# A decoder step on one core: column strips for the modulation projection, and gated-recurrence scores in two 64-token blocks

## The reference

```python
mod = jnp.einsum('bd,de->be', jax.nn.silu(c), w_ada[l]) + b_ada[l]     # 9 conditions, 1024 -> 6144
h = x * (1.0 + sc1) + sh1
...
scores = jnp.einsum('bhik,bhjk,bhijk->bhij', qi, ki, decay)            # decay = exp(b_i - b_j), j <= i
o = jnp.einsum('bhij,bhjv->bhiv', scores, vi) + jnp.einsum('bhik,bhkv->bhiv', qi * jnp.exp(b), s)
```

## Time and profile before

| | us |
|---|---|
| median of 3 runs | 2076.36 (2075.5 to 2076.95) |
| the profiled execution's own time | 2077.7 |
| its span, first to last instruction | 2075.9 |
| PE busy | 1972.5 (95%) |
| DVE busy | 696.5 (34%) |
| ACT busy | 445.5 (21%) |
| POOL busy | 420.5 (20%) |

### The profile page before, as it was taken

One profiled execution on the slowest core, in us unless ns is written; L12 is line 12 of the kernel. 1 busy time (PEld: TensorE's weight loads), 2 busy tenths in 40 slices (PEclk: granted clock), 3 DMA queues, 4 the chain that ended last, 5 costly groups with the idle time before them and its releaser, 6 DMA issues.

```text
span 2075.9 us, 24423 instructions
## 1 busy us (share of the span) xinstructions
PE 1972.5 (95%) x7628; PEld 1224.6 (59%) x7628; DVE 696.5 (34%) x1473; ACT 445.5 (21%) x946; POOL 420.5 (20%) x661
## 2 busy tenths in 40 slices
PE   6999999999999999999969999999999999999994
PEld 1754548587858757888857444444444444444443
DVE  1113980499049943000147411111111111111114
ACT  1203431344134443000021111111111111111111
POOL 0001430144014300000000612222222222222220
PEclk9899999999999989999978899999999999999997
DMA  9112432200220083311021599999999999999962
GB/s 387 41 41 85 161 127 84 81 27 19 83 81 2 4 325 123 145 59 41 9 80 62 203 388 372 362 374 364 375 362 372 358 373 368 364 372 360 377 178 93
DMA packets 56941, 419.50 MB, mean 202 GB/s; under 512 B 6289, under 2 KB 10001, under 8 KB 31145
## 3 DMA queue, kind: packets, MB, share of 16 engines
q1 hardware_dynamic: 33689, 339.44, 40.8%
q0 software_dynamic: 21456, 78.10, 14.5%
q10 hardware_dynamic: 1728, 1.05, 0.2%
HBM read 362.96 MB, written 55.61 MB: 202 GB/s over the span
## 4 chain that ended last, share of the span: by engine, by line
PE 83%; DVE 9%; ACT 3%; issue 2%; POOL 1%; DMA 1%; SPq 0%; POOLq 0%; DVEq 0%; ACTq 0%
PE ps L1023 24%; PE ps L1045 12%; PE ps L885 11%; PE ps L846 8%; PE ps L831 7%; PE ps L1014 3%; PE ps L917 3%; PE ps L776 2%; DVE work L1419 2%; PE ps L466 2%; DVE Xb L1426 1%; PE ps L802 1%; PE ps L984 1%; ACT work L572 1%; ACT work L570 1%
## 5 line engine op out<-in xcount | busy, mean ns | idle before, releaser
L1023 PE MATMUL ps<-W,work 128*128 128x512 f32 x1168 | 515.8, 595 | 1.5 <-ACT work L1206 1.2
L1023 PEld LDWEIGHTS ps<-W,work 128*128 128x128 f32 x1168 | 217.1, 191 | 247.9 <-issue 247.9
L1045 PE MATMUL ps<-work 128*128 128x512 f32 x576 | 259.1, 592 | 0.0
L1725 DVE SCALAR_TENSOR_TENSOR work<-ps,work 128x256 f32<-128x256 f32 x73 | 35.3, 484 | 514.5 <-ACT work L1212 514.5
L846 PE MATMUL ps<-Hb,W 128*128 128x260 f32 x768 | 173.4, 389 | 0.0
L1045 PEld LDWEIGHTS ps<-work 128*128 128x128 f32 x576 | 103.8, 190 | 103.3 <-issue 103.3
L846 PEld LDWEIGHTS ps<-Hb,W 128*128 128x128 f32 x768 | 148.7, 194 | 24.3 <-ACT work L1106 0.7
L1241 POOL TENSOR_TENSOR work<-work 128x128 f32<-128x128 f32 x168 | 83.0, 527 | 388.1 <-ACT work L572 388.1
L1735 DVE COPY work<-ps 128x512 f32<-128x512 f32 x144 | 99.6, 692 | 179.3 <-DMA ffrows<-work 92.5
L1311 POOL DMA_INDIRECT ffrows<-work x72 | 115.7, 1607 | 192.2 <-DVE work L1735 121.6
L831 PE MATMUL ps<-W,Hb 128*128 128x512 f32 (+1 forms) x320 | 138.4, 592 | 0.0
(11 more groups left out here) (250 smaller groups left out, 2177.0 us busy)
## 6 DMA issues: line engine op xcount, KB each, us to landing
W<-wexp SPq DMA_DIRECT2D x74, 2048.0 KB, 8.8
work<-wexp SPq DMA_DIRECT2D x73, 1024.0 KB, 8.0
W<-wq SPq DMA_DIRECT2D x36, 2048.0 KB, 8.2
work<-st_in SPq DMA_DIRECT2D x8, 1024.0 KB, 8.1
st_out<-work SPq DMA_DIRECT2D x8, 1024.0 KB, 7.3
Xb<-xT SPq DMA_DIRECT2D x2, 2080.0 KB, 17.3
h2rows<-work SPq DMA_DIRECT2D x5, 512.0 KB, 2.6
yT<-Xb SPq DMA_DIRECT2D x2, 1040.0 KB, 5.3
```

The lines of the kernel that those rows point to most:

```text
L1023: mm = pe.matmul(ps[:, k % 2, :], xe[:, k % 2, c, :], GU[:, k % 4, c, :], start=(c == 0), stop=(c == KC - 1))
L1045: mm = pe.matmul(ps[:, 4 + hf, :], aT[:, k % 2, f, :], WD[:, k, f, hf * 512:(hf + 1) * 512], start=(f == 0), stop=(f == 1))
```

## The change

- **Strips.** The 9 silu'd conditions are written into a zeroed table of 32 columns per chunk (`cond32`, in `OB`). `mod_proj` writes chunk c to partitions 32*(c%4) and up; two chunks accumulate in each of the four strips. ACT copies all 128 partitions, and `mod_turn` becomes a matmul with a 0/1 table `fold` (128x9) that adds the four strips while it turns.
- **Blocks.** The 128 tokens of a chunk are taken as two blocks of 64. Level 0 has only the corner (keys of the first block, queries of the second): one 64x64 product, which needs no mask and is copied by DVE to its place. Levels 1 to 6 and the diagonal are made for each block apart, 14 products of 64x64, each to the 64 partitions of its block. The other corner of the sum is zeroed once.
- **Layout.** The level is the innermost index of the results (in a bank: 64 tokens by 8 levels), so that a result of PE is written with a stride of 8 words, and the sum over the levels reads neighbours. A step uses bank 0 or 1 in turn, and `scores_of(n)` waits for `mask(n-2)`, no longer for `mask(n-1)`.
- The mask table shrinks from 1024 to 512 columns, the table of constants from 1930 to 1427.

```diff
 def mod_proj(n, chunks):
 ...
                 for c in chunks:
-                    mm = pe.matmul(ps[0:NCOND, mod_bank(n), :], conds[:, c, :], ring[:, q % 4, :, c, :],
-                                   start=(c == 0), stop=(c == KC - 1))
+                    strip = slice(32 * (c % 4), 32 * (c % 4) + 32)
+                    mm = pe.matmul(ps[strip, mod_bank(n), :], cond32[:, c, :], ring[:, q % 4, :, c, :],
+                                   start=(c < 4), stop=(c >= 4))
 ...
-                    mm = pe.transpose(ps[:, 5, at:at + NCOND], mod_rows(n)[:, u * P:(u + 1) * P], ident[0:NCOND, 0:NCOND])
+                    mm = pe.matmul(ps[:, 5, at:at + NCOND], mod_rows(n)[:, u * P:(u + 1) * P], C("fold"), start=True, stop=True)
 ...
 def scores_of(n):
 ...
-                since(pe, s_pm, n)
-                for l in range(LEV):
-                    pe.matmul(ps[:, l // 4, (l % 4) * CH:(l % 4 + 1) * CH], M[:, p, l, col_], M[:, p, l, col_],
-                              start=True, stop=True)
-                pe.matmul(ps[:, 1, 3 * CH:4 * CH], M[:, p, 9, col_], q4[:, h, cc * CH:(cc + 1) * CH],
-                          start=True, stop=True).then_inc(s_sc, 1)
+                since(pe, s_pm, n - 1)
+                out = levels[n % 2]
+                first, second = (slice(c * CH + r.start, c * CH + r.stop) for r in blocks)
+                pe.matmul(out[blocks[0], :, 7], M[:, p, 0, first], M[:, p, 0, second], start=True, stop=True)
+                for l in range(1, LEV):
+                    for r, at in zip(blocks, (first, second)):
+                        pe.matmul(out[r, :, l - 1], M[:, p, l, at], M[:, p, l, at], start=True, stop=True)
+                for r, at in zip(blocks, (first, second)):
+                    mm = pe.matmul(out[r, :, 6], M[:, p, 9, at], q4[:, h, cc * CH + r.start:cc * CH + r.stop],
+                                   start=True, stop=True)
+                mm.then_inc(s_sc, 1)
 ...
 def mask(n):
                     dve.wait_ge(s_sc, n + 1)
                     since(dve, s_st, n)
-                    dve.tensor_tensor(Pm, ps[:, 0:2, :].rearrange("p b t -> p (b t)"), C("masks"), ALU.mult).then_inc(s_pm, 1)
+                    dve.tensor_tensor(Pm, levels[n % 2][:, :, 0:7], C("masks").rearrange("p (t l) -> p t l", l=8)[:, :, 0:7],
+                                      ALU.mult)
+                    since(dve, s_o, n - 1)
+                    dve.tensor_copy(ST[blocks[0], n % 2, blocks[1]], levels[n % 2][blocks[0], :, 7]).then_inc(s_pm, 1)
                     dve.wait_ge(s_pm, n + 1)
-                    since(dve, s_o, n - 1)
-                    dve.tensor_reduce(ST[:, n % 2, :], Pm.rearrange("p (l t) -> p t l", l=8), AX, ALU.add).then_inc(s_st, 1)
+                    for r in blocks:
+                        ins = dve.tensor_reduce(ST[r, n % 2, r], Pm[r], AX, ALU.add)
+                    ins.then_inc(s_st, 1)
```

More of the change, by code:

```diff
@@ L36 @@
 LEV = 7
+BL = CH // 2
 GH, GV = 4, 256
@@ L80 @@
                          ("wgk1", KC * RANK)])
-CONST, NCONST = columns([("ident", P), ("ones", P), ("mean", P), ("masks", 8 * P), ("reset", NT), ("mhalf", 1), ("eps", 1)])
+CONST, NCONST = columns([("ident", P), ("ones", P), ("mean", P), ("masks", 8 * BL), ("reset", NT), ("mhalf", 1), ("eps", 1),
+                         ("fold", NCOND)])
 ROUTE, NROUTE = columns([("tri", P), ("iota", P), ("group", NG), ("quads", MAXT // 4), ("part", 1),
@@ L96, in constants @@
     masks = []
-    for l in range(LEV):
+    jb, ib = j % BL, np.arange(BL)[None, :]
+    for l in range(1, LEV):
         s = CH >> (l + 1)
-        masks.append((j // (2 * s) == i // (2 * s)) & (j % (2 * s) < s) & (i % (2 * s) >= s))
-    masks.append(j == i)
-    put(CONST, c, "masks", np.stack(masks, 1).reshape(P, 8 * P))
+        masks.append((jb // (2 * s) == ib // (2 * s)) & (jb % (2 * s) < s) & (ib % (2 * s) >= s))
+    masks += [jb == ib, np.zeros((P, BL))]
+    put(CONST, c, "masks", np.stack(masks, 2).reshape(P, 8 * BL))
     t = np.arange(NT)
@@ L104, in constants @@
     put(CONST, c, "mhalf", -0.5)
+    put(CONST, c, "fold", (j % 32 == np.arange(NCOND)[None, :]))
     put(CONST, c, "eps", EPS)
@@ L141, in decoder_step @@
         tiny = sb("tiny", 256)
-        ints = sb("ints", 256, I32)
+        ints = sb("ints", 128, I32)
         ps = ctx.enter_context(nc.psum_tensor("ps", [P, 8, 512], F32))
@@ L167, in decoder_step @@
         conds = S("cond").rearrange("p (c n) -> p c n", c=KC)
+        cond32 = view(OB, 0, KC * 32, "p (c n) -> p c n", c=KC)
         V = view(work, 0, 4096, "p (t n) -> p t n", t=NCH)
@@ L177, in decoder_step @@
         qrows = view(Xb, 1088, 12 * DEC * 32, "p (h n) -> p h n", h=12)
-        Pm = view(Xb, 2336, 1024)
+        Pm = view(Xb, 2336, 7 * BL, "p (t l) -> p t l", l=7)
+        blocks = [slice(0, BL), slice(BL, CH)]
+        levels = [ps[:, b, :].rearrange("p (t l) -> p t l", l=8) for b in range(2)]
         ST = view(Xb, 3360, 256, "p (b t) -> p b t", b=2)
@@ L414, in mod_rows @@
         def mod_rows(n):
-            return view(work, 512 * n, 512)[0:NCOND, :] if n < 4 else side[0:NCOND, 0:512]
+            return view(work, 512 * n, 512) if n < 4 else side[:, 0:512]
         def mod_bank(n):
@@ L497, in recurrence_pe @@
             pe.wait_ge(s_zev, taken(gi, "v"))
+            pe.wait_ge(s_zst, 1)
             scores_of(base)
@@ L764, in _ @@
             pe.wait_ge(s_small, 48)
-            pe.wait_ge(s_cs, 1)
+            pe.wait_ge(s_cs, 2)
             def quad_ready(q):
@@ L1074, in _ @@
             act.wait_ge(s_small, 48)
-            act.activation(conds, conds, ACT.Silu).then_inc(s_cs, 1)
+            act.wait_ge(s_cs, 1)
+            act.activation(cond32[:, :, 0:NCOND], conds, ACT.Silu).then_inc(s_cs, 1)
             def copy_rows(n):
@@ L1082, in copy_rows @@
                     act.wait_ge(s_z, taken(0, "g"))
-                act.activation(mod_rows(n), ps[0:NCOND, mod_bank(n), :], ACT.Copy).then_inc(s_mr, 1)
+                act.activation(mod_rows(n), ps[:, mod_bank(n), :], ACT.Copy).then_inc(s_mr, 1)
             for n in range(4):
@@ L1318, in _ @@
         def _(dve):
+            dve.memset(cond32, 0.0).then_inc(s_cs, 1)
             dve.wait_ge(s_small, 48)
@@ L1353, in _ @@
             dve.tensor_tensor(H[:, :, SEQ:NT], H[:, :, SEQ:NT], md[:, SH1:SH1 + 8, 1:NCOND], ALU.add).then_inc(s_h, 1)
+            dve.wait_ge(s_h, 9)
+            dve.memset(ST[blocks[1], :, blocks[0]], 0.0).then_inc(s_zst, 1)
             for gi in range(3):
```

1 line of the change is left out of this document (added).

## The result

The changed kernel takes 2029.7 us (median of 4 runs, 2028.67 to 2031.06), the kernel before 2075.9 (with a fourth run): a ratio of 0.978 (95% interval 0.9766 to 0.9795). The forecast was 2033, in a range of 2020 to 2052. The profiled execution took 2028.67 us, its span is 2026.8.

A forecast was written before the change was run, and what follows sets the result against it. PE alone was taken to bound the start, with DVE setting the groups' pace. Start -12.6, group 0 -15.6, groups 1 and 2 -15.0 made -43.2 us: from 2077.7 profiled to 2034.5, as a median 2033, range 2020 to 2052.

The forecast's parts named there:

- Start, -12.6: Start up to the first projection: quads of 1.9 us instead of 7.0, projections at 35.2; -12.6 us, bounds -13.4 and -11.5.
- so 30.2: Start: X lands at 4.09 + 26.7 = 30.8, less 0.6 us for the smaller table of constants, so 30.2.
- Score block, 1.75: Scores on PE: weight loads set 30 passes at 1.63, with the passage 1.75 us against 1.77 before; nothing gained.
- Mask and sum, -1.27: DVE's mask, copy and two sums, now reading neighbours, take 1.87 us instead of 3.14; -1.27 a step.
- Group 0, -15.6: Group 0 in all: five cycles -6.3, head -5.1, tail -4.2, together -15.6 us.
- 15.45 - 1.27 = 14.2: Middle of group 0: DVE sets the `mq` to `mq` cycle, which falls to 14.2 us; five cycles, -6.3.
- Group 1, -7.5: Group 1: cycle 14.77 - 1.27 = 13.5 us, five cycles -6.3, one mask-and-sum at the tail -1.2; -7.5.
- Group 2, -7.5: Group 2, taken as alike to group 1 and costed like it: -7.5 us.
- The sums did not stay slow: Rival, 14%: DVE's sums still cost 1.8 ns an element because of short runs, some 10.5 us over 48 steps; 2044.
- half-width passes are not full ones: Rival, 5%, claimed the opposite: half-width passes cost a full pass, score block 3.45 us; 2089, slower.
- strips do not stream in single file: Rival, 5%, claimed the opposite: strips stream one after the other, no gain at start or fills; 2055.
- The clock did fall in group 0: Rival, 18%: PE, waiting more, drops to clock 0.50 in group 0; all of it loses 22 us, half assumed; 2044.

The follow-up runs named there:

- x_first: Changed kernel, but SP issues the fifth to eighth quads only after X has landed; 2032.5 us, ratio 0.9796.
- halves_apart: Changed kernel, but the twelve level passes of one half are issued in a row, then the other half's, not in turn; 2034.8 us.
- fill_clock: Changed kernel plus six unused 384-column PE passes before every second score block of group 0; 2039.4 us, ratio 0.9827.
- blocks_only: Changed kernel without the strips: 64-token blocks alone, modulation projection in one strip as before; 2046.6 us, ratio 0.9864.
- sums_stride: Changed kernel with masked products laid level by level, so the sums read with a stride of 64 elements; 2049.2 us, ratio 0.9874.
- fill_short: Changed kernel plus three unused 384-column PE passes before every second score block of group 0; 2031.1 us, ratio 0.9792.
- scale_late: Changed kernel, but in group 0 ACT does Abs and Exp ahead of scaling the previous output, in steps with both; 2025.5 us.
- strips_only: Kernel before plus only the strips of the modulation projection, scores as before; 2069.1 us, ratio 0.9967.

## Why the prediction was right, and where it was not

The total came out close, 46.2 us gained in the medians against 43.2, in part by luck: the columns of the two traces add up to 49.1, and several terms missed in opposite directions.

**Start, -12.6: -10.9 at the first projection, -14.4 at the first mask.** The step that failed is X's landing "so 30.2": 32.65 was measured, which puts the first projection outside its bound. "Behind X" held for the quads (x_first). What did not carry over is the 26.7 of the earlier trace rows as a fixed time: it is 26.7 to 29.6 in the fourteen traces, in the two lengths told above. They follow neither the later quads (x_first) nor whether DVE waits (it does in halves_apart, 26.8, and does not in fill_clock, 28.3). A quad of 1.9 at full clock and the half quad of 1.00 (measured 0.99 to the next instruction) were right. The 3.5 us gained between the projection and the first mask were not predicted: 1.7 of them lie in the two short projections, whose clock varies (L840 took 6.51 before, L856 takes 4.92), 1.1 in the long ones behind them, and 0.7 in the first score block. The 1.7 are luck: blocks_only, which leaves PE's work at the start as it was, shows as much there.

**Score block, 1.75: 1.07 (to the start of the next matmul).** The step that failed is "The weight loads set more ... 30 of them 1.63". Taken one half at a time this is near (58 ns a pass instead of 54, and 1.59 for the block in halves_apart, where some passes still pair up); in turn, loads and passes of the halves overlap, and the time lies near the lower bound of 0.95. "Nothing gained on PE" is thus 0.7 a step where PE leads, as at the first mask, which follows the end of the last projection by 2.14 us instead of 2.83.

**Mask and sum, -1.27: -1.09.** Mask 0.61, copy 0.20, sums 0.61 each, all as forecast; the term was 0.18 too large, since the four overlap less than I took. That it was the stride that made the old sums slow is shown by sums_stride.

**Group 0, -15.6: -15.3, with errors that cancel.** "DVE sets the cycle" is shown by blocks_only, whose five cycles are as long as those of the changed kernel in spite of half quads of 3.53. "15.45 - 1.27 = 14.2" is what a cycle with a held root does (14.4, with the measured 1.09); I did not see that the root in this chain could also slip through, which two cycles of 13.45 did; that is luck, and the five cycles gave 7.1 instead of 6.3. The head gave 5.9 instead of 5.1. The tail was over-estimated: -4.2 forecast, -2.3 measured, and nothing or worse from the strips alone. DVE leads there too, and the last turn, costed at "some 0.4 more", takes 1.56 us to the next matmul instead of 0.35, at a granted clock of 0.50, that is 1.2 GHz, where it was 1.00 (before, then now):

```profile
315.31 0.41 PE L785 MATMUL ps<-cst,side 9*128 9x9 f32 x4
...
284.52 1.72 PE L801 MATMUL ps<-cst,side 128*128 128x9 f32 x8
```

**Group 1, -7.5: -7.3. Group 2, -7.5: -10.6.** Group 1's chain is the one forecast, but its cycle is 13.84, not 13.5:

```profile
411.63 3.13 DVE L1439 TENSOR_TENSOR work<-work 128x128 f32<-128x128 f32 x7 [0.95 <-ACT work L587]
...
425.47 3.13 DVE L1439 TENSOR_TENSOR work<-work 128x128 f32<-128x128 f32 x7 [1.01 <-ACT work L587]
```

The five cycles gave 4.8 instead of 6.3. That the sum is right all the same is luck: from the first mask to the third `mq`, where nothing was forecast, it gained 1.0, and the tail gave 1.5 instead of 1.2. "Group 2 is alike" is the step that failed. Before, its cycles were 15.29 and 14.2 in turn, the long ones with the root held (2.07 us); now all take 13.2 to 13.3, and the root is through in 0.19 or 0.38. Its first half before and now, in such a place:

```profile
671.64 2.07 POOL L1247 TENSOR_SCALAR tiny<-tiny 128x1 f32<-128x1 f32 x1 [3.24 <-ACT Xb L603]
...
616.47 0.38 POOL L1264 TENSOR_SCALAR tiny<-tiny 128x1 f32<-128x1 f32 x1 [2.07 <-ACT Xb L618]
```

**Rivals.** The sums did not stay slow, half-width passes are not full ones, and strips do not stream in single file (1.07 us for eight passes). The clock did fall in group 0, to 0.91, as that rival had it and against the 1.00 that was to show the forecast right; but its price was not half of 22. It is at most 0.95 in each of the three long cycles and 1.2 in the last turn; with the clock back at 1.00 no cycle is shorter (fill_short), and with the root off the chain 0.87 costs a cycle nothing (scale_late). In strips_only the middle is 1.6 longer, 1.2 of it in the one cycle with the lowest clock.

## What to carry to other kernels

Where an engine seems to wait for a short instruction of another (here 0.19 us on POOL that took 0.46 or 1.46), look for what runs at that moment on the engine that may lock it out; here a change of order that takes it off the chain gained 5.7 us with one moved line. Sum over the innermost index in SBUF and let PE write the layout that this wants. PE, made faster than the chain, paid with its clock (0.91 instead of 1.00 in group 0) and gained only where it led: at the start and at the head of one group. And compare two blocks of passes over the same ends: to the last pass's start or to the next matmul's.

## What the runs showed of the hardware

- POOL's 0.19 us instruction, started 1.352 to 1.355 us after DVE's first subtraction, was held 1.46 us in fill_short, and was through in 0.46 in the changed kernel; scale_late and blocks_only show both. What decides is open: the starts differ by no more than 3 ns.
- 64x64 passes in alternate halves start in pairs, 4 or 5 ns apart, every 58 ns; in one half they start one by one, 58 ns apart.
- A 128x448 mask written to SBUF with a stride of 64 elements took 0.93 us instead of 0.61; read from PSUM with that stride it took 0.61.
- X, 2080 KB at the end of a full queue, landed 19.6 to 19.7 us after the first quad in six traces and 20.8 to 21.2 in eight; later transfers on the queue made no difference (x_first). Why is open.
